# Input projections of a two-layer hybrid encoder in three fp32r steps from high and low parts, in place of two fp32 steps

## The reference, cut to what matters

```python
h = rms_norm(x, W['norm_mix'][l])
gq, gk, gv, gr, ga, hq, hf, hi, hgate, rx, rgate = jnp.split(h @ W['w_in'][l], points, axis=-1)
o_gla, sg = gla_mixer(gq, gk, gv, gr, ga, ...)
o_hg, sh = hgrn2_mixer(hq, hf, hi, hgate, ...)
o_rg, sr, sc = rglru_mixer(rx, rgate, ...)
x = x + jnp.concatenate([o_gla, o_hg, o_rg], axis=-1) @ W['w_out'][l]
```

## Time and profile before

| | |
|---|---|
| median of 3 timed runs | 1727.54 us (1723.6 to 1727.8) |
| the profiled execution's own time | 1722.73 us |
| its span, first to last instruction | 1720.5 us |
| busy share of the span | PE 98%, PEld 88%, DVE 64%, ACT 54%, POOL 6% |
| chain that ended last | PE 95%, ACT 2%, DVE 2%, issue 1% |
| mean granted clock of TensorE | 0.992 |
| layer 0: first input product, first key product | 17.91 us, 149.07 us |
| layer 1: first input product | 558.26 us |

### The profile page before, as it was taken

One profiled execution on the slowest core, in us unless ns is written; L12 is line 12 of the kernel. 1 busy time (PEld: TensorE's weight loads), 2 busy tenths in 40 slices (PEclk: granted clock), 3 DMA queues, 4 the chain that ended last, 5 costly groups with the idle time before them and its releaser, 6 DMA issues.

```text
span 1720.5 us, 32188 instructions
## 1 busy us (share of the span) xinstructions
PE 1689.9 (98%) x13385; PEld 1509.4 (88%) x13385; DVE 1109.5 (64%) x1236; ACT 930.3 (54%) x1071; POOL 101.8 (6%) x152
## 2 busy tenths in 40 slices
PE   7999999999999999999999999999999999999997
PEld 6788889999999777988888999999999999999996
DVE  5156516455544235623548888788888878888798
ACT  2334624444432133543357777676777767677675
POOL 3000210110001000101010000000000000000000
PEclk9999999999999999989999999999999999999999
DMA  8126363255457423426189999999999999999992
GB/s 216 56 76 197 106 193 132 80 173 171 155 146 186 104 74 106 164 56 224 63 294 325 365 317 374 317 369 366 323 366 324 374 316 369 367 325 366 322 365 89
DMA packets 356674, 400.60 MB, mean 233 GB/s; under 512 B 24892, under 2 KB 329688, under 8 KB 356584
## 3 DMA queue, kind: packets, MB, share of 16 engines
q1 hardware_dynamic: 345488, 381.58, 67.7%
q0 software_dynamic: 6176, 15.27, 2.5%
q10 hardware_dynamic: 4920, 2.43, 0.5%
HBM read 387.66 MB, written 11.58 MB: 232 GB/s over the span
## 4 chain that ended last, share of the span: by engine, by line
PE 95%; ACT 2%; DVE 2%; issue 1%; DMA 0%; DVEq 0%; SPq 0%; ACTq 0%
PE ps L683 93%; ACT ring L1218 1%; PE ps L1147 1%; PE ps L970 0%; ACT low L1218 0%; DMA ring<-in_x_sample_dram 0%; DVE dw_lo L1632 0%; DVE w_lo L2062 0%; PE ps L766 0%; ACT kvw_hi L1218 0%; PE ps L902 0%; DVE att L1934 0%; ACT L1218 0%; PE ps L844 0%; ACT rstd L1218 0%
## 5 line engine op out<-in xcount | busy, mean ns | idle before, releaser
L2062 DVE TENSOR_TENSOR w_lo<-ring,w_hi 128x2048 fp32r<-128x2048 f32 x264 | 604.1, 2291 | 101.3 <-ACT w_hi L1218 93.7
L1218 ACT ACTIVATE w_hi<-ring 128x2048 fp32r<-128x2048 f32 x264 | 504.5, 1914 | 126.9 <-PE ps L683 126.8
L683 PE MATMUL ps<-w_hi,hg_hi 128*96 128x256 f32 x1408 | 396.7, 282 | 2.3 <-DVE hg_lo L2051 2.3
L683 PE MATMUL ps<-w_hi,hg_lo 128*96 128x256 f32 x1408 | 395.2, 281 | 0.0
L683 PE MATMUL ps<-w_lo,hg_hi 128*96 128x256 f32 x1408 | 394.4, 280 | 0.0
L683 PEld LDWEIGHTS ps<-w_hi,hg_hi 128*96 128x96 f32 x1408 | 228.8, 162 | 7.3 <-issue 2.5
L683 PEld LDWEIGHTS ps<-w_lo,hg_hi 128*96 128x96 f32 x1408 | 227.9, 162 | 5.0
L683 PEld LDWEIGHTS ps<-w_hi,hg_lo 128*96 128x96 f32 x1408 | 229.3, 163 | 0.0
L1632 DVE TENSOR_TENSOR dw_lo<-ring,dw_hi 128x2048 fp32r<-128x2048 f32 (+1 forms) x54 | 113.1, 2094 | 106.5 <-ACT dw_hi L1218 106.5
L1218 ACT ACTIVATE low<-ps 96x256 f32<-96x256 f32 (+7 forms) x164 | 63.3, 393 | 186.9 <-PE ps L683 185.7
L1218 ACT ACTIVATE dw_hi<-ring 128x2048 fp32r<-128x2048 f32 (+1 forms) x54 | 94.6, 1753 | 109.7 <-PE ps L683 82.7
(11 more groups left out here) (310 smaller groups left out, 2675.6 us busy)
## 6 DMA issues: line engine op xcount, KB each, us to landing
ring<-in_moe_w_dram SPq DMA_DIRECT2D x264, 1024.0 KB, 6.9
ring<-in_ffd_w_dram SPq DMA_DIRECT2D x22, 1024.0 KB, 5.2
ring<-in_ffd_w_dram SPq DMA_DIRECT2D x16, 704.0 KB, 4.5
ring<-in_w_in_dram SPq DMA_DIRECT2D x14, 768.0 KB, 4.3
ring<-in_w_in_dram SPq DMA_DIRECT2D x8, 1024.0 KB, 5.7
ring<-in_xa_wk_dram SPq DMA_DIRECT2D x8, 1024.0 KB, 5.2
ring<-in_xa_wv_dram SPq DMA_DIRECT2D x8, 1024.0 KB, 6.0
ring<-in_xa_wq_dram SPq DMA_DIRECT2D x8, 1024.0 KB, 4.9
```

Of the source, the lines that this page charges most:

```text
L683: return nc.tensor.matmul(out, lhsT, rhs, start=first, stop=last)
L1218: return nc.scalar.activation(out, in_, func, **kw)
L2062: V.tensor_tensor(view(w_lo, off, SLOT), view(ring, moe_slot(u) * SLOT, SLOT), view(w_hi, off, SLOT).bitcast(F32), ALU.subtract).then_inc( ...
```

## The change

All input projections but the values (12 of the 33 input chunks of a layer) take the split form. Each layer's weight units for rx, rgt, hf, ga with two gates, hq and the other six gates, and the two halves of `wqk`, get a high part in one of two new places, which lie over the buffers of the memory keys and values (`kp`, `vp`), and a low part in the slot, or, for q and k, in a place over `b_t` and `kl_t`. `hT` is split too: ACT copies each tile to `in_hi` (over `sq`), and DVE subtracts into `in_lo` (over `a_full`). So POOL's clearing of `a_full` moves behind the last gate, the memory tokens move to another address, the two high places of the memory weights change their order, and the first of them waits for the last value. One list, `SEQ`, now says which operand is split next. Its main parts:

```diff
-        SPLIT_UNITS = [n for n, unit in enumerate(units) if unit[0] != "in" and unit[0] != "out"]
+        def is_split(key, l, a, b):
+            return key != "out" and not (key == "in" and (GV <= a < GR or HI <= a < HGT))
+        SEQ = []
+        for n, unit in enumerate(units):
+            if is_split(*unit):
+                SEQ.append(n)
+            if unit[0] == "in" and unit[2] == RGT:
+                SEQ += [("qk", unit[1], 0), ("qk", unit[1], 1)]
...
-                pool.wait_ge(chunk_ready, CHUNK_NO[("dn", 7) if l else ("mem", 3)] + 1)
+                pool.wait_ge(chunk_ready, CHUNK_NO["gate", 8 * l + 7] + 1)
...
-            def project(tag, w, m0, m, rhs, n, fresh=None):
-                        pe.wait_ge(normed, NORMED[fresh] + k + 1)
-                    last = mm(ps[0:m, b, 0:n], w[:, k, m0:m0 + m], rhs[:, k, 0:n], k == 0, k == KD - 1)
+            def project(tag, w, m0, m, fresh=None):
+                        pe.wait_ge(in_split, KD * fresh + k + 1)
+                    last = split_mm(ps[0:m, b, 0:T], w[0][:, k, m0:m0 + m], w[1][:, k, m0:m0 + m],
+                                    in_hi[:, k, :], in_lo[:, k, :], k == 0, k == KD - 1)
...
             for l in range(LAYERS):
+                if l:
+                    act.wait_ge(kv_stored, 16 * 2 * l)
+                else:
+                    unit_hi()
                 norm(3 * l, added("dn", 0) if l else lambda d: act.wait_ge(resid_done, 1),
-                     {d: 2 for d in range(KD - 1)} if l else {})
+                     {d: 2 if d < KD - 1 else 1 for d in range(KD)} if l else {})
+                for k in range(KD):
+                    act.wait_ge(normed, NORMED[3 * l] + k + 1)
+                    f(in_hi[:, k, :], hT[:, k, :], ACT.Copy).then_inc(in_hi_done, 1)
+                unit_hi()
...
+            def norm_lo(l):
+                for k in range(KD):
+                    dve.wait_ge(in_hi_done, KD * l + k + 1)
+                    V.tensor_tensor(in_lo[:, k, :], hT[:, k, :], in_hi[:, k, :].bitcast(F32), ALU.subtract
+                                    ).then_inc(in_split, 1)
...
             for l in range(LAYERS):
+                if l == 0:
+                    unit_lo()
                 norm(3 * l, c_mix + 8 * l)
+                norm_lo(l)
+                unit_lo()
```

More of the change, by code:

```diff
@@ L438, in layer_program @@
         ATT_LAST = CHUNK_NO["ox", 8 * LAYERS - 1] + 1
-        SPLIT_UNITS = [n for n, unit in enumerate(units) if unit[0] != "in" and unit[0] != "out"]
+        def is_split(key, l, a, b):
[6 more added lines that the diff above has]
+                SEQ += [("qk", unit[1], 0), ("qk", unit[1], 1)]
+        KINDS = []
+        for entry in SEQ:
+            key = "in" if isinstance(entry, tuple) else units[entry][0]
+            KINDS.append({"in": "in", "wk": "kv", "wv": "kv", "out": "out"}.get(key, "dw"))
+        NTH = [KINDS[:m].count(kind) for m, kind in enumerate(KINDS)]
+        PLACE_BEFORE = [next((p for p in range(m) if KINDS[p] == kind and NTH[p] == NTH[m] - 2), None)
+                        for m, kind in enumerate(KINDS)]
         H_BASE = {1: 0, 2: 2 * KD, 4: 3 * KD}
@@ L453, in unit_used, with split_used, hi_place, split_words @@
                 eng.wait_ge(chunk_ready, unit_last[n] + 1)
[L455 to L459, removed]
+        def split_used(eng, m):
+            if isinstance(SEQ[m], tuple):
+                _, l, i = SEQ[m]
+                eng.wait_ge(chunk_ready, CHUNK_NO["qk"[i], 2 * l + 1] + 1)
+            else:
+                unit_used(eng, SEQ[m])
+        def hi_place(m):
+            return {"in": inw_hi, "kv": kvw_hi, "dw": dw_hi}[KINDS[m]][NTH[m] % 2]
+        def split_words(m):
+            if isinstance(SEQ[m], tuple):
+                return SLOT
+            key, l, a, b = units[SEQ[m]]
+            return STEPS * P if key == "w2" else KD * (b - a) if key == "in" else SLOT
+        def split_source(m):
+            if isinstance(SEQ[m], tuple):
+                return wqk[:, SEQ[m][2], :, :].rearrange("p k n -> p (k n)")
+            return slot(SEQ[m], split_words(m))
+        def lo_place(m):
+            if isinstance(SEQ[m], tuple):
+                return view(wqk_lo[SEQ[m][2]], 0, SLOT)
+            return view(dw_lo, (SEQ[m] % DSLOTS) * SLOT, split_words(m))
         def slot(n, *dims):
@@ L1988, in _ @@
                                             ALU.subtract).then_inc(ff_split, 1)
-                    add_residual("dn", {d: 2 for d in range(KD - 1)}, scaled=True)
+                    add_residual("dn", {d: 2 if d < KD - 1 else 1 for d in range(KD)}, scaled=True)
             V.memset(htok[:, 2, :], 0.0).then_inc(htok_zero, 1)
```

94 lines of the change are left out of this document (59 added, 35 removed).

## The result

The changed kernel takes 1734.11 us (median of 10 runs, 1731.45 to 1738.41) against 1725.89 us of the kernel before (10 runs, 1720.35 to 1731.65). The ratio is 1.0053, 95% interval 1.004 to 1.0065. The profiled execution has a span of 1730.4 us in place of 1720.5. The mean granted clock of the changed kernel's ten executions lies between 0.977 and 0.984, so that the number of slow stretches differs between executions; the profiled one has 0.984 and is the second fastest.

A forecast was written before the change was run, and what follows sets the result against it. PE, busy 98% of the span, bounds the kernel; its work falls 29.4 us, mostly repaid in waits. Layer 0 +9.2 and layer 1 -8.2 give +1.0 us on the 1720.5 us span, 1728.5 us as median; range 1720.5 to 1736.

The forecast's parts named there:

- second rival: Layer 1 and gates: hand-offs use up the slack, subtractions make PE or a take wait, 9.1 us, 1737.6 us; chance 0.22.
- fall one: Layer 0's sums of squares: the clock drops to half after PE idles about 7 us, costing 1.5 us.
- margin of hf's or the gates' low parts: hf's low part has 0.5 us to spare in layer 1; the gates' lie in DVE's idle 5.54 us.
- first rival: Whole kernel: the clock does not fall, so 1721.2 us, or 1720.5 us; chance 0.25.
- Layer 0 ends 9.2 us late: Layer 0's sum: ga 15.7 us late, less 3.5 for five chunks and 3.0 for two gate pairs.
- Fall two: Layer 0's rx: after PE idles 5 us the clock drops to half, costing 1.5 us.
- fall four: Layer 0 before ga: PE waits about 3 us for the memory norm, then half clock costs 1.5 us.
- forecast's factor (1 - 0.1335/0.24): Share of a half-clock stretch lost, from 288-column steps of 0.24 us in place of 0.1335; 3.4 us costs 1.5.
- From ga on: Layer 0, ga to keys: five chunks run without a wait, 3.5 us back; two gate pairs give 3.0 back.
- DVE's chain: End of layer 0's gates: exp to first key weight's low part, 11.5 us unshrinking; third pair's gain becomes PE's wait.

The follow-up runs named there:

- kernel with layer 1 alone: Against the kernel before: only layer 1's input projections are split, layer 0 keeps its fp32 steps; 1716.08 us, ratio 0.9949.
- kernel with the shift in waits: Changed kernel plus unused 64x32 products behind the sums of squares, 36 in layer 0 and 28 in layer 1; 1726.72 us, ratio 1.0010.
- A shift by 128 of the profile's matmuls: Changed kernel plus 64 unused products of 64x32 ahead of TensorE's first transposes; 1734.01 us, ratio 1.0062.
- shift of 200 at the start: Changed kernel plus 100 unused products of 64x32 ahead of TensorE's first transposes; 1730.24 us, ratio 1.0036.
- kernel with the load held back: Changed kernel, but layer 0's third key weight is issued only when the last level group is finished; 1732.47 us, ratio 1.0039.
- k and memory moves alone: Changed kernel, but in layer 0 k's and hf's low parts and the memory norm are pulled forward; 1719.73 us, ratio 0.998.

## Why the prediction was right in its parts and short in its size

It forecast 1728.5 us and no change, in a range that reaches to 1736. The time lies 5.6 us above the forecast and, by a little, beyond what it called no change. It is still inside the range, and that is luck: the range went up to 1736 for the second rival's sake, whose waits did not come.

Right were these steps. The first step came at 30.1 (29.7 forecast), with the squares at 18.55 us behind a second table load (18.34); the sums of the squares took 5.99 us where the kernel before takes 4.15, 1.84 more for fall one (1.5 forecast). k waited 3.41 us for its low part (3.5), the memory transposes 3.33 us behind ACT (3). In layer 1 PE waited nowhere between rx and hq, and from its sums of squares (18.7 us late) to its keys (11.2 late) it gained 7.5 us, 8.2 forecast, although the slow stretch behind its first wait lasted 6.8 us and not 3.4 (from 579.2 us); the kernel with layer 1 alone gives the same as a whole time. No margin of hf's or the gates' low parts failed, so the second rival did not happen, although its time of 1737.6 was the nearer one. The first rival did not happen either: the clock fell.

The clearing of a_full at its new place cost DVE nothing. DVE's and POOL's rows beside it:

```profile
157.31 1.36 DVE L1944 TENSOR_TENSOR ring<-ring 128x1152 f32<-128x1152 f32 x1
157.38 2.66 POOL L657 MEMSET ring<- 128x3072 f32 x1 [138.43 <-PE ps L725]
158.58 2.29 DVE L1693 TENSOR_TENSOR dw_lo<-ring,kvw_hi 128x2048 fp32r<-128x2048 f32 x1
```

2.29 us is the low part's usual time. The trace agrees with the Trainium skill (SBUF — State Buffer, SBUF: two separate sides), by which such a clearing does not hold up a DVE operation with two SBUF inputs.

The step that failed is "Layer 0 ends 9.2 us late"; it is 14.1 at the keys and 18.7 at layer 1's sums of squares. Three terms of it were mis-sized.

1. **"Fall two" to "fall four" at 1.5 us each.** The size of one fall was right: the windows show stretches at 0.50 that last 3.4 us. But some last 6.8, and there were more of them. Counted in windows of 1 us, layer 0 of the changed kernel has 3.4 us behind 29 us, 6.8 behind k, 3.4 behind 74, 3.4 behind the stall, and 3.4 and 6.8 at 213 and 224 us: 27.2 in place of three times 3.4. By the forecast's factor (1 - 0.1335/0.24) the 17.0 us too many cost 7.5. k's stretch shows it; by the forecast it ends at 57.7 us:

```profile
58.00:59.00 1.00, 1.00 (x6) 1.00 (x6) 0.98 (x4) 0.00 (x0) 0.00 (x0) 0.50 0.00 0
59.00:60.00 1.00, 1.00 (x6) 1.00 (x6) 0.86 (x5) 0.00 (x0) 0.00 (x0) 0.50 0.00 0
60.00:61.00 1.00, 1.00 (x8) 1.00 (x8) 1.00 (x1) 0.41 (x1) 0.00 (x0) 0.82 0.00 0
```

Fall one is not among these stretches. Its windows (length, PE's busy us and steps, the granted clock, DMA share and GB/s) show a clock of 1.00, and yet PE's steps in the first are twice as long as in the second:

```profile
20.00:20.50 0.50, 0.50 (x2) 1.00 1.00 327
23.50:24.00 0.50, 0.50 (x4) 1.00 1.41 166
```

In the kernel with the shift in waits the same sums, 6.86 us long, have a clock of 0.50 up to 24.6 us. So the changed kernel's row of the clock seems to leave out a slow stretch at its start, and the mean of 0.95 above is then a little too high.

The kernel before has one such stretch of 3.4 us of its own at 304 us, which the changed one lacks, so that by the same factor 1.5 us come back before layer 1.

2. **"From ga on" counted no standstill but that of DVE's chain.** The two stalls inside the level groups are 0.70 and 3.59 us. DVE's chain alone would have let the keys begin at 158.58 + 2.29 + 0.11 = 160.98 us; the stall makes it 163.18, 2.2 more, and the half clock behind it (term 1) comes on top. No row of before has more than 0.55 of it, and that one is DVE's too: no step of the prediction could have read it there, though one could have asked what 50% more matmuls a chunk do to PE's supply.

3. **The end of layer 0's sum at the keys.** The late key weight (1.68 us of PE at 182.04) lies behind it.

7.5 + 0.70 + 2.2 + 1.68 - 1.5 = 10.6 us, 1.1 more than the 9.5 by which 18.7 exceeds 9.2. It is an estimate: the factor is that of 288-column steps back to back. The stretches at 213 and 224 us, for one, cost 3.7 us and not the 4.5 that it gives: between the same two steps of the memory's projections (from 197.14 us before, from 214.20 in the changed kernel) 20.85 us go by in place of 17.11.

Layer 1 and what follows gave back a little more than forecast (the end is 8.8 us less late than layer 1's sums, 8.2 forecast).

## What to carry to other kernels

When a change cuts an engine's work but adds preparation on others, read their order of work before their load: here moving three pieces on ACT and DVE was worth 1.1% of the time, twice the loss. Count a standstill of the matmul engine at its own length and the slow stretch behind it, and allow that stretch two or three times the length of the one seen. A standstill called "issue" that stands behind the same instruction in every kernel is to be tested by shifting the instruction stream, with products placed in a wait that exists.

## What the runs showed of the chip

PE can stop for 2.2 to 4.1 us inside a group of small matmuls that wait for nothing. In six executions without a shift (of the changed kernel and five variants) it was after 133 of 144 in layer 0. A shift by 128 of the profile's matmuls left it there (after 134), two by 72 (mod 128) removed it, and with the shift of 200 at the start a stall appeared in layer 1. In these long stalls a packet of the queue that the page calls instruction is on its way; the row is the 0.25 us from 160.00 of the changed kernel, in which the key weight's load fills the DMA engines:

```profile
q1 hardware_dynamic: 95, 0.10, 109.2%
q8 instruction: 1, 0.02, 27.3%
```

The packet has 16 KB and is on its way from 160.22 to 161.31 us; PE goes on at 162.73. Read like this, all traces agree: of the 23 standstills of over 0.1 us between small products, in ten kernels, every one ends 1.0 to 1.6 us after such a packet of that queue has landed (in layer 1 of the kernel with layer 1 alone the packet ends at 678.82 and PE goes on at 679.86). The load of the key weight shows in the packet's start: in the six traces with that load the packet begins 2.6 to 3.0 us after the group's first product, in the kernel with the load held back 1.24 us, and it is on its way for 1.2 us there, 0.9 to 1.6 in the six. That PE's instructions ran out fits all of this, since 128 matmuls with their weight loads pass in 1.6 us there; whose instructions the packet holds no row says, so the supply is inferred, and the dependence on position and the tie to the packets are what was shown.

Open is why the clock fell at 213 and 224 us of the changed kernel, where PE had no standstill: most kernels with layer 0 split show one or two such stretches there, but the one with the k and memory moves alone and the one with the held load none, and neither do the kernel before and the one with layer 1 alone. Open, too, is why some stretches last 3.4 us and others 6.8 or, in seven of the kernels, 10.2: k's took 6.8 in the changed kernel and 3.4 in the one with the shift in waits, behind the same standstill of 3.4 us.
